# Bias tiles loaded in order, a shorter routing chain, mixes in the last units and the seldom path first: a two-layer encoder trunk with experts on one core

## The reference

```
for layer in range(2):
    h = rmsnorm(x, norm_mix[layer]);  proj = h @ w_in[layer]      # q, k, v of two mixers, gate logits
    # mixer A: 8 heads, 64-frame chunks, 9-chunk key band, bias by clipped distance:
    idx    = clip(query - key, -128, 128) + 128
    scores = q k^T / 8 + rel_bias[head][idx];   ya = softmax(scores) @ v
    # mixer B: 8 query heads on 2 key heads, 2-chunk band, ALiBi slopes, a sink per head
    x = x + (sigmoid(g0) * (ya @ w_branch_a) + sigmoid(g1) * (yb @ w_branch_b)) @ w_out
    h = rmsnorm(x, norm_ffn[layer])
    if layer == 0: x = x + (silu(h @ w_gate) * (h @ w_up)) @ w_down          # width 2816
    else:                                                                   # 8 experts of width 1408
        top_v, top_i = top_k(h @ w_router, 2);  top_w = softmax(top_v)
        x = x + sum over the two chosen e of top_w * swiglu_e(h)
return rmsnorm(x, norm_final)
```

## Time and profile before

| | us |
|---|---|
| median of 3 runs | 1630.04 (1628.44 to 1630.43) |
| the profiled execution, whole | 1628.77 |
| its span in the trace | 1627.0 |
| PE busy in the span | 1594.3 (98%) |
| DVE busy | 1016.4 (62%) |
| ACT busy | 845.0 (52%) |
| POOL busy | 241.4 (15%) |

### The profile page before, as it was taken

The page is one execution under the profiler, slowest core; times in us unless marked ns, Lnnn a source line. Parts: engine busy times, 40 slices in busy tenths (PEclk is TensorE's granted clock), DMA queues, the critical chain, the costliest instruction groups (busy, mean ns, idle before and its releaser), DMA issues.

```text
span 1627.0 us, 22853 instructions
## 1 busy us (share of the span) xinstructions
PE 1594.3 (98%) x7705; PEld 1329.9 (82%) x7706; DVE 1016.4 (62%) x1689; ACT 845.0 (52%) x1309; POOL 241.4 (15%) x295
## 2 busy tenths in 40 slices
PE   9999999999999999999999999999999999999997
PEld 6788888788888888888888887878788888888885
DVE  6646765654444443345467657756567898876675
ACT  5436664342322232233366653565557878875653
POOL 2004663000000000011035640010101100110001
PEclk9999999999999999999999999999999999999999
DMA  6432122244443333344321224166768999996771
GB/s 206 122 110 66 56 66 78 92 130 155 142 145 115 104 88 93 105 119 131 107 66 59 66 78 144 64 242 216 225 217 269 364 369 368 359 335 222 219 305 54
DMA packets 86331, 263.13 MB, mean 162 GB/s; under 512 B 12445, under 2 KB 20637, under 8 KB 85728
## 3 DMA queue, kind: packets, MB, share of 16 engines
q1 hardware_dynamic: 79072, 245.45, 45.3%
q0 software_dynamic: 7168, 16.54, 3.6%
HBM read 240.50 MB, written 17.08 MB: 158 GB/s over the span
## 4 chain that ended last, share of the span: by engine, by line
PE 89%; DVE 6%; issue 2%; ACT 2%; DMA 1%; ACTq 0%; SPq 0%; POOL 0%; PEldq 0%; DVEq 0%; POOLq 0%
PE ps L1550 18%; PE ps L1551 17%; PE ps L1552 17%; PE ps L1892 7%; PE ps L1894 6%; PE ps L1893 6%; PE ps L1890 4%; PE ps L1891 4%; PE ps L1732 2%; PE ps L1765 1%; DVE m_lo L1065 1%; PE ps L1745 1%; PE ps L1764 1%; PE ps L1744 1%; PE ps L1872 1%
## 5 line engine op out<-in xcount | busy, mean ns | idle before, releaser
L1065 DVE TENSOR_TENSOR m_lo<-m_raw,m_hi 128x1024 fp32r<-128x1024 f32 (+1 forms) x280 | 318.7, 1160 | 101.6 <-ACT m_hi L780 97.8
L780 ACT ACTIVATE m_hi<-m_raw 128x1024 fp32r<-128x1024 f32 (+1 forms) x280 | 279.5, 1010 | 165.4 <-PE ps L1891 129.9
L1550 PE MATMUL ps<-h_hi,w_hi 128*128 128x512 f32 x888 | 354.0, 399 | 1.6 <-DVE w_lo L1060 1.6
L740 ACT ACTIVATE w_hi<-raw 128x1024 fp32r<-128x1024 f32 (+1 forms) x169 | 177.1, 1048 | 328.0 <-PE ps L1552 325.2
L1551 PE MATMUL ps<-h_lo,w_hi 128*128 128x512 f32 x888 | 346.8, 391 | 0.0
L1552 PE MATMUL ps<-h_hi,w_lo 128*128 128x512 f32 x888 | 346.6, 390 | 0.0
L1060 DVE TENSOR_TENSOR w_lo<-raw,w_hi 128x1024 fp32r<-128x1024 f32 x137 | 165.7, 1210 | 135.6 <-ACT w_hi L740 134.8
L1552 PEld LDWEIGHTS ps<-h_hi,w_lo 128*128 128x128 f32 x888 | 166.7, 188 | 35.6
L1550 PEld LDWEIGHTS ps<-h_hi,w_hi 128*128 128x128 f32 x888 | 167.1, 188 | 28.0 <-issue 2.7
L1551 PEld LDWEIGHTS ps<-h_lo,w_hi 128*128 128x128 f32 x888 | 167.5, 189 | 26.2 <-issue 0.7
L1892 PE MATMUL ps<-m_hi,xt_hi 128*128 128x512 f32 (+1 forms) x384 | 144.6, 377 | 5.8 <-DVE m_lo L1065 3.9
(11 more groups left out here) (272 smaller groups left out, 2916.6 us busy)
## 6 DMA issues: line engine op xcount, KB each, us to landing
m_raw<-moe_g SPq DMA_DIRECT2D x128, 512.0 KB, 5.7
m_raw<-moe_down SPq DMA_DIRECT2D x88, 512.0 KB, 4.9
raw<-w_in SPq DMA_DIRECT2D x68, 512.0 KB, 3.6
m_raw<-moe_g SPq DMA_DIRECT2D x64, 384.0 KB, 4.6
raw<-w_gu SPq DMA_DIRECT2D x44, 512.0 KB, 3.6
raw<-w_out SPq DMA_DIRECT2D x16, 512.0 KB, 3.6
raw<-w_down SPq DMA_DIRECT2D x16, 512.0 KB, 3.5
raw<-w_a SPq DMA_DIRECT2D x8, 512.0 KB, 3.5
```

The costliest lines, as they stand in the source:

```text
L740: A.activation(split_of(n, 0, cols)[0], raw[:, n % RAW, 0:cols], ACT.Copy).then_inc(hi_ready, 1)
L780: A.activation(m_hi[:, u % M_SPL, 0:cols], m_raw[:, u % M_RAW, 0:cols], ACT.Copy).then_inc(m_hi_ready, 1)
L1065: V.tensor_tensor(m_lo[:, u % M_SPL, 0:cols], m_raw[:, u % M_RAW, 0:cols], m_hi[:, u % M_SPL, 0:cols].bitcast(F32), ALU.subtract).then_inc ...
L1550: E.matmul(ps[:, bank, :], wh, hi, start=first, stop=False)
```

## The change

What it does, part by part:

- **Bias.** Two new copies from DRAM to DRAM on SP's queue, behind units 7 and 9 of layer 0, write every row of `rel_ext` 128 times to `rel_rows` (786 KB for each layer). POOL loads `bias` from there in the right order, ACT reads it from SBUF, and `turn_bias` and `flip` go.
- **Router.** `w_hi` of that unit holds the high part (8 columns) beside the low part (8 columns), so that PE needs two matmuls for each k instead of three. DVE sums the two halves after the transposes.
- **Turn of h.** ACT writes `h` in float32 (`h32`, 8 operations of 128x512 in the `w_out` units named in `H32_AT`), and `turn_h` is 32 plain transposes. All four tiles stand ahead of the ranks; a third pair of PSUM banks takes the third tile.
- **Lists.** The 16 columns of the first round are made and summed first, the other 32 later. Two `turn_x` tiles stand ahead of the sums.
- **Turned rows.** The second slot has PSUM banks of its own (`TURN_BANKS`), and a section begins unit 0 when the first slot is split.
- **Mixes** move from units 18 to 25 to units 25 to 33.
- **Placement** runs over slots outside and halves inside.
- **Branches.** In SP, POOL, ACT and DVE the path for `most` over `CAP` stands first, and the other path, reached by a jump, ends the program without a branch inside.

```
+REL = 3 * P
+REL_AT = (7, 9)
...
+        def h32(k):
+            if k < 2:
+                return gf_row[:, k * T:(k + 1) * T]
+            n = MIX_START[DEPTH - 1] + U_OUT + 5 + (k - 2) // 2
+            return raw[:, n % RAW, k % 2 * T:(k % 2 + 1) * T]
+        H32_AT = ((0,), (1,), (), (), (2,), (3,), (4, 5, 6), (7,))
...
-        PREMIX = {18 + m: (m // 2, m % 2) for m in range(2 * TT)}
+        PREMIX = {25: (0,), 27: (1,), 29: (2,), 30: (3,), 31: (4,), 32: (5,), 33: (6, 7)}
...
+        TURN_BANKS = (0, 4)
...
-            return (0, 4)[t % 2]
+            return (0, 4, 6)[t % 3]
...
+                    if layer == 0 and u in REL_AT:
+                        i = REL_AT.index(u)
+                        sp.dma_start(rel_rows[i], bass.AP(tensor=rel_ext.tensor, offset=i * HEADS * REL, ap=[[REL, HEADS], [0, P], [1, REL]])
+                                     ).then_inc(rel_copied[i], 16)
...
-                    pool.wait_ge(bias_turned, i)
+                    pool.wait_ge(bias_ready, i // HEADS * 2 * HEADS + i % HEADS)
...
-                pool.dma_start(bias[:], bass.AP(tensor=rel_ext.tensor, offset=i * 384, ap=[[1, P], [1, 2 * P]])).then_inc(bias_in, 16)
+                pool.wait_ge(rel_copied[i // HEADS], 16)
+                pool.dma_start(bias[:], bass.AP(tensor=rel_rows.tensor, offset=i * P * REL + P - 1, ap=[[REL - 1, P], [1, 2 * P]])
+                               ).then_inc(bias_in, 16)
...
-                A.wait_ge(bias_turned, layer * HEADS + hh + 1)
-                A.activation(bias_t[:, H % 2, 2 * P:T], ps[:, bank, 2 * P:], ACT.Identity,
+                A.wait_ge(bias_masked, layer * HEADS + hh + 1)
+                A.activation(bias_t[:, H % 2, 2 * P:T], bias, ACT.Identity,
...
-                    if layer == 0 or n + 2 <= last:
+                    if layer == DEPTH - 1 and n + 2 == last:
+                        A.wait_ge(raw_full[last % RAW], 16 * (last // RAW + 1))
+                        A.wait_ge(unit_done, last - SPL + 1)
+                        A.activation(router_parts()[0], router_raw, ACT.Copy).then_inc(hi_ready, 1)
...
+                    if layer == DEPTH - 1:
+                        for k in H32_AT[u]:
+                            if k >= 2 and k % 2 == 0:
+                                A.wait_ge(lo_ready, n0 + U_OUT + 5 + (k - 2) // 2 + 1)
+                            A.activation(h32(k), xs[:, k, :], ACT.Copy, scale=gains[:, gain_of(norm_i + 1), k:k + 1]).then_inc(h32_ready, 1)
...
+            halves_of = ps[:, 2, :].rearrange("p (t c) -> p t c", c=P)[:, :, 0:2 * EXPERTS].rearrange("p t (i e) -> p t e i", e=EXPERTS)
+            link(V.tensor_reduce(key, halves_of, AX.X, ALU.add))
+            link(V.tensor_tensor(lg, key, each(rinv[:, 3, :]), ALU.mult))
...
+            columns(0, SOON)
+            V.wait_ge(rows_turned, TT)
             for c in range(2):
                 mine = slice(c * TT, (c + 1) * TT)
-                V.tensor_tensor(entry_hit[:, mine, :, :], in_column[:, mine, :].unsqueeze(3).to_broadcast([P, TT, LISTS, 2]),
-                                entry[:, mine, :].unsqueeze(2).to_broadcast([P, TT, LISTS, 2]), ALU.mult)
+                entries(c, 0, SOON)
                 V.tensor_tensor(row_hit[:, mine, :], numbers[:].unsqueeze(1).to_broadcast([P, TT, P]),
...
+            V.wait_ge(lists_summed, 2)
+            later = ps[:, 3, 0:2 * (LISTS - SOON)].rearrange("p (c i) -> p c i", i=2)
+            V.tensor_scalar(lists[:, SOON:LISTS, 0], later[:, :, 0], float(PAD_H), None, ALU.add)
+            link(V.tensor_scalar(lists[:, SOON:LISTS, 1], later[:, :, 1], float(PAD_Y), None, ALU.add))
+            V.sem_inc(lists_ready, 1)
...
-                        mix(*PREMIX[u], 0)
+                        for m in PREMIX[u]:
+                            mix(m // 2, m % 2, 0)
...
-            with V.If(V.value_load(counts[0:1, LAST:N_SEC], min_val=0, max_val=T) > P):
-                section(0, LAST, SLOTS, last=True)
-                with V.If(crowded <= CAP):
...
             with V.If(crowded > CAP):
+                with V.If(V.value_load(counts[0:1, LAST:N_SEC], min_val=0, max_val=T) <= P):
+                    section(0, LAST, 1, last=True)
+                with V.Else():
+                    section(0, LAST, SLOTS, last=True)
...
+            with V.Else():
+                with V.If(V.value_load(counts[0:1, LAST:N_SEC], min_val=0, max_val=T) <= P):
+                    section(0, LAST, 1, last=True)
+                    norm_placed()
+                with V.Else():
+                    section(0, LAST, SLOTS, last=True)
+                    norm_placed()
...
-                    E.wait_ge(rows_copied, t - 1)
+                if t >= 3:
...
-                    out = ps[:, x_bank(t) + k // 4, (k % 4) * P:(k % 4 + 1) * P]
-                    E.matmul(out, h_hi[:, k, t * P:(t + 1) * P], ident_r[:], start=True, stop=False)
-                    mm = E.matmul(out, h_lo[:, k, t * P:(t + 1) * P], ident_r[:], start=False, stop=True)
-                mm.then_inc(rows_turned, 1)
+                    if t == 0:
+                        E.wait_ge(h32_ready, k + 1)
+                    tr = E.transpose(ps[:, x_bank(t) + k // 4, (k % 4) * P:(k % 4 + 1) * P], h32(k)[:, t * P:(t + 1) * P], ident[:])
...
-                def turn_bias(hh, bank):
-                    i = layer * HEADS + hh
-                    E.wait_ge(bias_masked, i + 1)
-                    E.matmul(ps[:, bank, 2 * P:], flip[:], bias, start=True, stop=True).then_inc(bias_turned, 1)
...
+                both = w_hi[:, U_ROUTER % SPL, k * P:k * P + 2 * EXPERTS]
+                E.wait_ge(h_lo_ready, 3 * KD + k + 1)
+                E.matmul(ps[0:2 * EXPERTS, LOGIT_BANK, :], both, h_hi[:, k, :], start=k == 0, stop=False)
+                mm = E.matmul(ps[0:2 * EXPERTS, LOGIT_BANK, :], both, h_lo[:, k, :], start=False, stop=k == KD - 1)
...
             E.wait_ge(logits_ready, 1)
             for t in range(TT):
...
...
+            turn_x(1)
+            keep_warm(5, 2)
...
+            sum_lists(2, 0, SOON, (1, 2))
             E.wait_ge(counts_ready, 1)
-            for t in range(TT):
-                turn_x(t)
-            def turn_rows(done, sl, p16):
...
+            sum_lists(3, SOON, LISTS, (3, 3))
...
+            def turn_rows(sl, p16):
...
-                        E.wait_ge(xt_lo_ready, done + (k // 4 + 1))
-                    tr = E.transpose(ps[:, k // 4, (k % 4) * P:(k % 4 + 1) * P], xg[:, sl, k * P:(k + 1) * P], ident[:])
+                    tr = E.transpose(ps[:, TURN_BANKS[sl] + k // 4, (k % 4) * P:(k % 4 + 1) * P], xg[:, sl, k * P:(k + 1) * P], ident[:])
...
+            turn_rows(0, 16)
+            keep_warm(2)
+            turn_rows(1, 16)
...
-                        E.wait_ge(xt_lo_ready, i * 4 + (4 * first + 4))
+                        E.wait_ge(xt_lo_ready, i * 4 + (4 * first + 2))
...
+                                    if u == 0 and sl:
+                                        E.wait_ge(xt_lo_ready, i * 4 + (4 * first + 4))
...
-                        for sl in range(slots):
-                            if t == 0:
...
+                    for sl, half in itertools.product(range(slots), range(2)):
```

More of the change, by code:

```diff
@@ L1 @@
+import itertools
 from contextlib import ExitStack
@@ L475, in _ @@
             sp.wait_ge(counts_ready, 1)
-            with sp.If(sp.value_load(most[0:1, 0:1], min_val=0, max_val=T) <= CAP):
-                send_out()
-            with sp.Else():
+            with sp.If(sp.value_load(most[0:1, 0:1], min_val=0, max_val=T) > CAP):
                 sp.wait_ge(m_lo_ready, N_SEC * M_UNITS)
@@ L486, in _ @@
                     load_rows(t, y_more)
+                send_out()
+            with sp.Else():
                 send_out()
@@ L719, in first_rows @@
                 pool.tensor_scalar(first_out, first_out, r1[:, 6, 0:1], None, ALU.mult).then_inc(pool_out, 1)
-            with pool.If(pool.value_load(most[0:1, 0:1], min_val=0, max_val=T) <= CAP):
-                first_rows()
-            with pool.Else():
+            with pool.If(pool.value_load(most[0:1, 0:1], min_val=0, max_val=T) > CAP):
                 moves(N_SEC, MORE_SEC, y_more)
@@ L728, in _ @@
                 pool.sem_inc(moe_done, 1)
+                first_rows()
+            with pool.Else():
                 first_rows()
@@ L1038, in _ @@
             crowded = A.value_load(most[0:1, 0:1], min_val=0, max_val=T)
-            with A.If(A.value_load(counts[0:1, LAST:N_SEC], min_val=0, max_val=T) > P):
-                section(0, LAST, SLOTS, last=True)
-                with A.If(crowded <= CAP):
-                    norm_rows()
-            with A.Else():
-                section(0, LAST, 1, last=True)
-                with A.If(crowded <= CAP):
-                    norm_rows()
             with A.If(crowded > CAP):
+                with A.If(A.value_load(counts[0:1, LAST:N_SEC], min_val=0, max_val=T) <= P):
+                    section(0, LAST, 1, last=True)
+                with A.Else():
```

(24 more changed lines are left out.)

126 lines of the change are left out of this document (65 added, 61 removed).

## The result

| | changed | before | ratio |
|---|---|---|---|
| median of the runs, us | 1610.55 (4 runs, 1607.96 to 1615.13) | 1630.24 (4 runs, 1628.44 to 1630.72) | 0.9884 (0.9866 to 0.9902) |
| the profiled execution, us | 1607.96, span 1606.1 | 1628.77, span 1627.0 | |

The kernel is 19.7 us faster in the median (1.2%). The forecast was 1612.0, so the total is right. Of the 20.9 us between the two spans, the forecast terms gave 17.35 for a forecast of 17.45; another 3.5 came from places that the sum had at nothing, and a part of that is luck, as the rows show. Two repeats on other occasions gave medians of 1613.33 and 1610.48.

What follows compares the result with a forecast made beforehand. PE, busy 98% of the span, was taken as the bound. Terms of -7.0, -5.5, -4.6 and -0.35 sum to -17.45, 1611.3 for an execution like the profiled one; the median was put at 1612.0, range 1609.8 to 1617.7.

Steps and rivals of the forecast that it cites:

- Flips: In attention, 16 turns of bias leave PE's stream at 0.44 us each: 7.0 us less, bounds 6.0 to 7.5.
- Routing: Routing stage, with fewer router matmuls, shorter list sums and plain transposes of h: 5.5 us less, bounds 3.2 to 6.2.
- The 0.3 from transposes of 16 columns: In the routing stage, DVE's chain was to gain 0.3 us from narrower transposes; an estimate, with nothing as bound.
- the later of both is the lists: Before the gather, lists ready at 1062.6 were to end behind h's rows at 1062.0, putting the gather at 1063.45.
- Mixes: Last section: five mixes leave DVE's stream ahead of `m_act`, PE's 3.39 us wait falls to 0.2: 4.6 less, bounds 3.2 to 4.8.
- the clock's share: Behind the `m_act` wait, seven matmuls start 0.23 apart instead of 0.43, if the wait lowered the clock: 1.4 us less.
- Placement: At PE's 0.47 us wait for `y_last_lo`, half 1 of slot 0 goes before it: 0.35 less, bounds 0 and 0.5.
- Branch order: Seldom path first, the other a jump away, for four engines once or twice: 0 us, bound above 2.1.
- two jumps of 2.1 leave room: At the last section's start, DVE and ACT's jumps, priced from a 2.13 us PE gap, were to stay hidden.
- The 11.35 us to unit 5: In a two-slot last section, PE needs the split made at its start only 5 x 10 x 0.227 = 11.35 us later.
- jumps stall: Rival, chance 0.03: two instruction fetches that nothing hides, at the end, up to 2.1 us each, giving 1616.
- Copies: The two `rel_ext` copies in DRAM, 8.4 us each, cost nothing; each may take 15.5 us without loss.

## Why the prediction was right, and where it wasn't

- **Flips**, 7.0: 6.98 between the traces, 6.3 in the medians of the part alone. Right, step and size.
- **Routing**, 5.5 (3.2 to 6.2): 5.14. Right in size: router 1.74 for 1.8, gather 4.3 for 4.5, from gather to section 0.83 for 1.0. Two of its steps were not. The 0.3 from transposes of 16 columns wasn't there: DVE comes to its first operation behind them 0.07 earlier than the router accounts for. In its place DVE's wait for the ranks fell from 0.53 to 0.21, which the sum didn't have, and `in_column` came 1.9 earlier as forecast. That is luck. And h's last transfer was priced at the 2.60 of the earlier trace rows, where the transfers were further apart: it took 3.5 with all parts and ended just ahead of the lists, so "the later of both is the lists" held by 0.1 and not by 0.6. In the routing part alone it took 5.3 and was last, and the gain was 3.55.
- **Mixes**, 4.6: 4.6 alone in the medians, 4.9 in both traces. Right, the clock's share too.
- **Placement**, 0.35: 0.32.
- **Branch order**, 0, with bounds of 0 and 2.1: the step that failed, though its sum nearly holds. "What stands first is not run; the other path is a jump away" looked only at where the jumps go to, not at where they come from. The jump that was taken behind the last work is gone, and the end came 1.1 to 1.8 earlier in every kernel with the change in POOL, ACT and DVE (3.6 to 4.1 for 5.2 to 5.4); a gain should have been among the bounds. And "two jumps of 2.1 leave room" took its price from the nearest row, a wait of PE; ACT stood 4.8 to 7.1 us. The 11.35 us to unit 5 are right, but they count from PE's entry into the section. ACT and DVE have the end of the section ahead and the two splits to do in them, and 5.7 to 5.8 were left: PE waited 0 to 1.4, whatever was over that. The rival "jumps stall" was right that they stall, but put it at the end, where the new order is the shorter one, and at 2 x 2.1. The bound of 2.1 is also missing from the sum: 12.4 is the three low terms without it, and with it the upper end of the range would have been 1619.8. The Trainium skill's rule (page "Runtime: NRT & Kernel Launch", section "Instruction fetch mechanics"), that a taken branch out of the window has to fetch before the engine goes on, agrees with both ends: with the instruction packets in the last 9 us before, and with ACT's gaps now. It speaks for the change at one place and against it at the other. ACT's 0.76 at its one jump, over a longer path than either of the two, doesn't fit it.
- **Copies**, 8.4 us each: about 9.5 (packets from 26.5 to 36) and, beside POOL's transfers, 14 (40 to 54). Hidden, as forecast; the price was up to 1.7 times too small, and the second copy was close to the 15.5 that I gave as the limit. Two more of each did cost, but only at the second place.
- **Median against profiled execution**: the first profiled execution was the fastest of its four runs, by 2.5 us. What made it so isn't known, as the other three left no trace; the 1.85 us at the second section's start, where the clock happened not to fall, may be a part. The forecast of the median, 1612.0, lies among the medians of the three occasions (1610.5 to 1613.3).

## What to carry to other kernels

Where one engine is busy 98% of the time, take work out of its own stream and count it by the distance between starts: those terms came out within 0.4 us (one of them by two errors that cancelled). When branches are reordered, ask of every engine which jump is taken and what is behind it: a jump at the very end has nothing to hide behind, and one with a lead has only what is left of it after the work that stands between (here 5.8 us of 11.35), so that it becomes a wait in some executions. An independent transfer that ends just ahead of the critical one should be priced as a rival even when the sum calls it hidden, and priced for the spacing that the change gives it.

## What the runs showed of the hardware

- PE's wait at the second section's start was 1.88 to 3.55 us in 14 traces of kernels that differ elsewhere, and 1.88, 2.85 and 2.77 in three traces of one kernel. The profile names DVE's `m_lo`, which had been made before, and in two traces nothing; the starts of the later sections have waits of at most 0.4. Its cause was not tried.
- After that wait the granted clock fell to its lower level in some executions and not in others: it fell at 2.06, 2.13, 2.50, 2.85, 2.93, 3.08, 3.38 and 3.55 us, and did not at 1.88, 2.35, 2.43, 2.52, 2.67 and 2.77. After the 3.39 for `m_act` it fell in six of seven traces. A fall costs 1.4 to 2.6 us (7 to 13 matmuls at 0.43 for 0.23), and may with the wait's own spread be a good part of the 2 to 7 us between runs of one kernel, which was not shown: there is one trace for each.
- Two jumps stopped ACT for 4.8 to 7.1 us (6 traces), one jump for 0.76 us (1 trace). DVE stood 4.2 us at one jump (1 trace), and 5.1 to 7.0 at two in the three traces in which it was later than ACT's split; in the other three it waited for that split, for 4.9 to 7.1. What makes the difference between the engines is open.
- Where transfers of 512 KB follow each other at 1.0 us, with the 16 DMA engines busy all the time, the last one took 3.5 us in six traces, for 2.6 to 3.0 where they are further apart (6 traces).
